# Splitting the expert-weight loads of a one-core hybrid decoder step into halves, with a new cut of the last two units and one filler less

## The reference

```python
logits = (xt @ w_router + b_router).astype(jnp.float32)
top_v, top_i = lax.top_k(logits, TOP_K)          # 4 of 32
gates = jax.nn.softmax(top_v, axis=-1)
...
gu = xb @ w_gate_up[e] + b_gate_up[e]            # 1024 -> 2048
gate, up = gu[:, :D_EXPERT], gu[:, D_EXPERT:]
gate = jnp.minimum(gate, SWIGLU_LIMIT)
up = jnp.clip(up, -SWIGLU_LIMIT, SWIGLU_LIMIT)
act = (up + 1.0) * (gate * jax.nn.sigmoid(SWIGLU_ALPHA * gate))
return act @ w_down[e] + b_down[e]               # 1024 -> 1024
```

## Time and profile before

| | before |
|---|---|
| time, median of 3 runs | 1357.94 us (1357.71 to 1358.34) |
| profiled execution, its own time | 1358.47 us |
| its span, first to last instruction | 1356.8 us |
| TensorE busy | 1318.4 us, 97% |
| queue q1 (SP): bytes, share of 16 DMA engines | 460.21 MB, 84.0% |
| HBM read | 477.33 MB |
| mean granted TensorE clock | 0.996 |

### The profile page before, as it was taken

One profiled execution on the slowest core, in us unless ns is written; L12 is line 12 of the kernel. 1 busy time (PEld: TensorE's weight loads), 2 busy tenths in 40 slices (PEclk: granted clock), 3 DMA queues, 4 the chain that ended last, 5 costly groups with the idle time before them and its releaser, 6 DMA issues.

```text
span 1356.8 us, 16732 instructions
## 1 busy us (share of the span) xinstructions
PE 1318.4 (97%) x6850; PEld 728.7 (54%) x6850; DVE 417.3 (31%) x1089; ACT 258.0 (19%) x583; POOL 35.6 (3%) x56
## 2 busy tenths in 40 slices
PE   9999999999999999999999999999999999999997
PEld 8888888888887344344443443334334333434433
DVE  3755557885312221212111212112111112212112
ACT  2113374484202111010110110101011010101102
POOL 0000012110000000000000000000000000000000
PEclk9999999999999999999999999999999999999999
DMA  9445449997998999999999999999999999999995
GB/s 253 151 131 159 153 148 273 309 344 252 264 333 337 373 425 418 431 431 431 430 430 431 432 431 427 431 431 432 429 430 431 430 430 431 431 432 429 431 424 206
DMA packets 94709, 489.37 MB, mean 361 GB/s; under 512 B 8673, under 2 KB 73761, under 8 KB 78873
## 3 DMA queue, kind: packets, MB, share of 16 engines
q1 hardware_dynamic: 84896, 460.21, 84.0%
q0 software_dynamic: 4608, 24.41, 5.2%
q10 hardware_dynamic: 5129, 3.66, 1.0%
HBM read 477.33 MB, written 11.19 MB: 360 GB/s over the span
## 4 chain that ended last, share of the span: by engine, by line
PE 71%; DMA 27%; ACTq 0%; DVE 0%; issue 0%; ACT 0%; POOL 0%; SPq 0%; POOLq 0%; DVEq 0%
PE bank L320 70%; DMA plain_conv<-in_w_down 9%; DMA ring<-in_w_down 9%; DMA ring<-in_w_gate_up 6%; DMA plain_conv<-in_w_gate_up 3%; PE bank L971 2%; ACTq L691 0%; ACTq L689 0%; DVE exn L2022 0%; ACT plain_conv L937 0%; ACT ring L695 0%; ACT plain_conv L685 0%; SPq L377 0%; DVE exn L1555 0%; DVE plain_conv L2025 0%
## 5 line engine op out<-in xcount | busy, mean ns | idle before, releaser
L320 PE MATMUL bank<-ring,plain_conv 128*64 128x512 f32 (+1 forms) x1312 | 297.6, 594 | 13.9 <-DMA ring<-in_w_gate_up 13.7
L320 PE MATMUL bank<-exn,ring 128*128 128x264 f32 (+1 forms) x1168 | 262.2, 388 | 0.2 <-DVE exn L1555 0.2
L320 PEld LDWEIGHTS bank<-exn,ring 128*128 128x128 f32 (+1 forms) x1168 | 217.4, 189 | 40.3 <-issue 3.2
L320 PEld LDWEIGHTS bank<-ring,plain_conv 128*64 128x64 f32 (+1 forms) x1312 | 92.3, 137 | 190.3 <-issue 166.1
L320 PE MATMUL bank<-plain_conv 128*64 128x512 f32 (+2 forms) x848 | 185.3, 586 | 9.2 <-DMA plain_conv<-in_w_gate_up 8.8
L320 PE MATMUL bank<-ring,exn 128*64 128x512 f32 x576 | 127.6, 595 | 1.9 <-DMA ring<-in_w_down 1.9
L320 PEld LDWEIGHTS bank<-plain_conv 128*64 128x64 f32 (+2 forms) x848 | 59.3, 138 | 125.2 <-issue 109.0
L1950 DVE TENSOR_TENSOR xT<-xT,bank 128x264 f32<-128x264 f32 x128 | 54.4, 429 | 216.1 <-PE bank L320 214.4
L1956 DVE TENSOR_SCALAR bank<-bank 128x512 f32<-128x512 f32 x31 | 21.7, 700 | 321.1 <-PE bank L320 321.1
L320 PE MATMUL bank<-plain_conv,exn 128*64 128x512 f32 (+1 forms) x422 | 99.9, 590 | 2.1 <-DMA plain_conv<-in_w_down 1.8
L874 ACT ACTIVATE exn<-bank 128x512 f32<-128x512 f32 x31 | 18.5, 598 | 414.7 <-DVE bank L1956 414.7
(11 more groups left out here) (299 smaller groups left out, 842.0 us busy)
## 6 DMA issues: line engine op xcount, KB each, us to landing
ring<-in_w_gate_up SPq DMA_DIRECT2D x35, 4096.0 KB, 39.7
plain_conv<-in_w_gate_up SPq DMA_DIRECT2D x23, 4096.0 KB, 40.2
ring<-in_w_down SPq DMA_DIRECT2D x16, 4096.0 KB, 40.4
plain_conv<-in_w_down SPq DMA_DIRECT2D x11, 4096.0 KB, 39.0
ring<-in_w_in SPq DMA_DIRECT2D x36, 1024.0 KB, 5.4
ring<-in_w_gate_up SPq DMA_DIRECT2D x8, 2048.0 KB, 12.0
ring<-in_w_proj_b SPq DMA_DIRECT2D x8, 1024.0 KB, 9.9
plain_conv<-in_w_gate_up SPq DMA_DIRECT2D x4, 2048.0 KB, 12.5
```

The lines of the kernel that those rows point to most:

```text
L320: return nc.tensor.matmul(out, w, x, start=start, stop=stop)
```

## The change

Units 3 to 93 are all loaded in halves of 2 MB, each half issued when the half that it overwrites has been used. Units 94 and 95 come in four pieces of two rows each (1 MB, 8 KB in each partition), alternating between the two, instead of a half and two pieces by columns. TensorE takes them two rows at a time for both halves of the columns, and the last two rows for the left columns and then the right. The filler at line 1225 is removed.

```diff
-SPLIT = range(3, 11)
-HALVES = [sum(n % PLACES == q for n in (*SPLIT, 93)) for q in range(PLACES)]
+SPLIT = range(3, 94)
+ROWS_EACH = (48, 48, 32)
+HALVES = [sum(n % PLACES == q for n in SPLIT) for q in range(PLACES)]
...
-            def load_pair(p, m, q, first=0, split=(), final=False):
+            def load_pair(p, m, q, final=False):
                 j = PLACES * m + q
-                for c in range(first, UNITS):
+                for c in range(UNITS):
                     n = (q + c) % PLACES
                     used = 2 * UNITS * PAIRS * p + 2 * UNITS * j + 2 * (c - PLACES)
-                    if c in split or final and c == 3:
-                        for h in range(2):
-                            sp.wait_ge(S["w_used"], used + 1 + h)
-                            second = half_landed[n]
-                            load_half(j, c, n, h, second if h else unit_landed[n])
+                    if final and c >= 4:
+                        sp.wait_ge(S["w_used"], used + 2)
+                        load_rows(j, c, n, 0, 2, unit_landed[n])
                         continue
+                    sp.wait_ge(S["w_used"], used + 1)
+                    load_half(j, c, n, 0, unit_landed[n])
                     sp.wait_ge(S["w_used"], used + 2)
-                    if final and c >= 4:
-                        load_half(j, c, n, 0, unit_landed[n])
-                    else:
-                        load_unit(j, c, n)
+                    load_half(j, c, n, 1, half_landed[n])
                 if final:
-                    for h in range(2):
+                    for r in range(1, 4):
                         for c in (4, 5):
-                            load_columns(j, c, (q + c) % PLACES, h, columns_landed[h])
+                            load_rows(j, c, (q + c) % PLACES, 2 * r, 2 * r + 2, rows_landed[r - 1])
...
             pe.wait_ge(S["u_taken"], 2)
-            keep_busy(p_first[0], 2)
             pe.wait_ge(S["mark_ready"], 2)
...
                 def second_half(c):
                     n = UNITS * q + c
-                    if isinstance(m, int) and m == 0 and n in SPLIT:
-                        half_arrived(n % PLACES, 1 + sum(o % PLACES == n % PLACES for o in SPLIT if o < n))
-                    if final and c == 3:
-                        half_arrived(3, HALVES[3])
+                    if isinstance(m, int) and m == 0 and n < SPLIT[0]:
+                        return
+                    half_arrived(n % PLACES, UNITS * m + n // PLACES + (n % PLACES >= SPLIT[0]))
...
-                down_both(range(4), range(2), lambda x: arrived(4 + x))
-                down_both(range(4, KT), [0], columns_of(0)).then_inc(S["y_half"], 1)
-                down_both(range(4, KT), [1], columns_of(1)).then_inc(S["w_used"], 4)
+                down_both(range(2), range(2), lambda x: arrived(4 + x))
+                for r in (1, 2):
+                    down_both(range(2 * r, 2 * r + 2), range(2), rows_of(r))
+                down_both(range(6, KT), [0], rows_of(3)).then_inc(S["y_half"], 1)
+                down_both(range(6, KT), [1], rows_of(3)).then_inc(S["w_used"], 4)
```

More of the change, by code:

```diff
@@ L305, in build @@
         half_landed = [sem(f"half_landed{i}") for i in range(PLACES)]
-        columns_landed = [sem(f"columns_landed{i}") for i in range(2)]
+        rows_landed = [sem(f"rows_landed{i}") for i in range(3)]
         dve_step, pool_step = sem("dve_step"), sem("pool_step")
@@ L385, in load_rows @@
                 sp.dma_start(unit[n][:, D * r0:D * r1], unit_of(j, c)[:, r0:r1, :].rearrange("p s n -> p (s n)")).then_inc(landed, 16)
-            def load_columns(j, c, n, h, landed):
-                dst = unit[n][:, HALF:BIG].rearrange("p (s n) -> p s n", s=4)
-                sp.dma_start(dst[:, :, 512 * h:512 * h + 512], unit_of(j, c)[:, 4:8, 512 * h:512 * h + 512]).then_inc(landed, 16)
             for w, k in ((a["w_proj_a"], KT), (a["w_proj_b"], 2 * KT), (a["w_out"], KT)):
@@ L450, in load_pairs @@
                 sp.wait_ge(S["w_used"], 2 * UNITS * PAIRS * p + 2)
-                load_rows(0, 5, 0, 6, 8, columns_landed[1])
-                load_pair(p, 0, 1, split=range(5))
-                for q in range(2, PLACES):
+                load_rows(0, 5, 0, 6, 8, rows_landed[1])
+                for q in range(1, PLACES):
                     load_pair(p, 0, q)
@@ L1380, in down @@
                         if first and x and s == 2:
-                            pe.wait_ge(columns_landed[0], 48 * p + 16)
+                            pe.wait_ge(rows_landed[0], 48 * p + 16)
                         if s == 4:
@@ L1384, in down @@
                         if first and x and s == 6:
-                            pe.wait_ge(columns_landed[1], 48 * p + 16)
+                            pe.wait_ge(rows_landed[1], 48 * p + 16)
                         for half in range(2):
@@ L1400, in down_both, with rows_of @@
                     return ins
-                def columns_of(half):
+                def rows_of(r):
                     def landed_of(x):
-                        pe.wait_ge(columns_landed[half], 48 * p + 48)
+                        pe.wait_ge(rows_landed[r - 1], ROWS_EACH[r - 1] * (p + 1))
                         return unit[(q + 4 + x) % PLACES]
```

2 lines of the change are left out of this document (1 added, 1 removed).

## The result

The changed kernel takes 1364.42 us (median of 5 runs, 1361.87 to 1365.02) beside 1358.31 us for the kernel before (5 runs, 1357.71 to 1359.27). The ratio is 1.004, with a 95% interval of 1.0029 to 1.0051: slower by 6.1 us, or 0.4%. Forecast was 1364.5 us, in a range of 1360.2 to 1368.1. All ten executions lie inside the range, but the close match of the first median is luck: the terms of the sum were off by 1.2 to 2.1 us each, and the errors offset each other.

What follows compares the result with a forecast made beforehand. The DMA engines were taken to bound the kernel from 518 to 1311 us, TensorE after. Terms + 8.0 - 0.4 - 0.45 - 0.55 = + 6.6 us on a median of 1357.94 gave 1364.5 us, range 1360.2 to 1368.1.

Steps and rivals of the forecast that it cites:

- What bounds the kernel: From 518 to 1311 us the DMA engines' rate of moving units sets the time; after 1311 us TensorE does.
- Price of the halves: 82 newly halved units, 11 to 92, each cost 98 ns more per engine: + 8.0 us, bounds 4.8 and 10.7.
- estimate of 4.7 ns: Cost per extra packet worked out from the Trainium skill: 3.1 us for 656 extra packets of an engine.
- a time near 1359.6: Rival: the skill's cheaper packets end the sum at 1359.6 us; anything between 1355.9 and 1360.2 got 14 in 100.
- fixed 2 us: Rival: each transfer pays its own fixed time, serially 164 us for 82 more transfers; 1 in 100.
- What finer issue gives back: Halves issued earlier help only where the DMA queue ran dry, 504 to 518 us: - 0.4 us, bounds 0 and 1.4.
- the dry stretch: 504 to 518 us, DMA share 0.98 and 389 GB/s: 0.3 us lost by share, 1.4 by rate; 0.4 taken.
- The filler: Without the filler at 434.52 us, the gather, first units and DMA stream come earlier: - 0.45 us, bounds 0 and 0.65.
- The rival with the clock: TensorE's clock falls in the last two units, where there is no slack: 1.7 us more, 1366.2 us; 8 in 100.
- The end: After unit 92, the last pieces' landing decides; down matmuls end at 1352.0 us, 0.55 us less than the stream's delay.
- TensorE's lead: Sign: TensorE's lead over the arriving units is gone before 822 us.
- The first expert matmul: Sign: it starts 0.45 us earlier than 439.67 us.

Runs made afterwards that it cites:

- second measurement: The changed kernel run once more, nothing altered, for its spread and a second trace: 1360.82 us (5 runs) beside 1357.68 before, ratio 1.0035.

## Why the prediction was right, and where its terms were off

**What bounds the kernel: right.** From some 510 us the DMA engines set the time. Two kernels that differ from before only in the size of their packets end later by what the packets cost, to within 0.6 us (+ 6.8 where 656 x 9.4 ns are 6.2, + 17.95 where 1968 x 9.3 ns are 18.3).

**Price of the halves: mechanism right, size too high.** The term was + 8.0 us, 12.2 ns per extra packet. Measured are 9.4 ns, which is 82 x 8 x 9.4 = 6.2 us, and + 6.8 us for the whole kernel with smaller packets alone. The step that was mis-sized is the multiplication by the DMA share: a share over 100% over 770 us can hardly be anything but packets that overlap, and it makes small packets look dearer. The same working gives 13 ns per extra packet for those of 8 KB (1.010 x 12320 us for 40756 - 1235 packets), where the kernel's time rose by 17.95 / 1968 = 9.1 ns for each. By bytes, the row that the prediction priced from gives 45 x 16 x 0.032768 / 19.20 = 1228.8 ns against 1219.0, 9.8 ns. The estimate of 4.7 ns that was worked out after the Trainium skill, DMA: Bandwidth & Descriptors, section Why small descriptors are slow (HBM only), is half of what the runs show, and its rival, a time near 1359.6, did not come. The Trainium skill, DMA: Bandwidth & Descriptors, section Anatomy of one DMA, gives its fixed 2 us, from which the prediction made a rival, for the path of GpSimd's transfers, and these go by SP's; nothing of that size shows here (1229.1 against 1228.4 ns with twice the transfers).

**What finer issue gives back: too small.** The terms were - 0.4 for the dry stretch and - 0.55 at the end, together - 0.95 us. Packets alone cost + 6.8 us, halves with the same packets and filler + 4.45 (1362.07 against 1357.62): 2.35 us come back. With the old end the halves cost + 5.4 (1363.00), so about 1.4 us come back without the new end and up to 0.9 with it. The first part holds the dry stretch, for which the rate's bound of 1.4 us may have been nearer than the share, and TensorE following the last gate-and-up units by halves. How these two divide was not measured.

**The filler: wrong in kind.** The term was - 0.45 us, with "idle of a few tenths in their place I cost at nothing". Where the clock holds, the gain is there and larger than forecast: about 0.6 us in the traces (8.77 us from the router's 0.79 us group to the first expert matmul before, 438.77 - 430.62 = 8.15 in the second trace of the changed kernel). The lower group of the changed kernel, near 1360.7, lies 1.4 us under the one with the filler back. But in the first trace the clock falls right behind the filler's place, and by the two groups about half the executions do the same and end near 1364.4. The rival with the clock was written for the tail, at 1.7 us and 8 in 100. The fall came at the head, where TensorE's first matmuls free the places that the stream waits for: the DMA share is 0.48 instead of 0.78 from 436 to 444 us in the two traces, and the whole stream of units comes later. Between the two traces lie 3.8 us. The fall accounts for 3.0 of them; why the halves of unit 93 came another 0.8 us late is open.

**How the sum met the first median.** Against the times of before beside each, the packets cost + 6.8 instead of + 8.0, finer issue and the new end gave back 2.35 instead of 0.95, and the missing filler cost 6.1 - 4.45 = + 1.7 instead of - 0.45. Together this is + 6.1 beside the forecast + 6.6. The first two errors alone would have put the time 2.6 us under the forecast; the fall of the clock, which the sum lacked, made up for most of it. In the second measurement, with three of five executions in the lower group, the slow-down of 3.1 us is about half the forecast. (The low end of the range is 1357.94 + 2.2 = 1360.1, not 1360.2; nothing hangs on it.)

The Trainium skill, TensorE: Matmul & The Clock Gate, section Part 1: The HAM clock gate (the "warmup" mystery), gives the lower clock as that of an idle engine, and says of the rise from it that its moment varies between executions of one kernel. The traces here agree that executions of one program differ, for the fall too: with the filler gone it is there in one (0.57) and not in another (1.00). They differ from it in that TensorE wasn't idle but busy 4.64 of the 6 us ahead of the fall, where it was busy 5.21 with the filler. The kernel without either filler was busy 3.75 there, fell in its one trace and took 1362.75 us against 1357.68. All ten traces with both fillers have 1.00 from 436 to 444 us; of the four with one or both gone, two show a fall. That is the evidence for the fillers holding the clock; it is good but thin, as the kernel before without this one filler was no slower beyond the noise (ratio 1.0005) and didn't fall in its trace.

**The end: right in its lengths, lucky in its times.** Gate-and-up was forecast to end at 1331.9 and ended at 1331.54; the down matmuls at 1352.0, and ended at 1351.37, 5.97 us after those of before. These times hold for the execution with the fall, which the forecast didn't have; without it they are 1327.68 and 1347.49. The lengths are right in both: the last piece was forecast 20.1 us behind unit 93's second half and came 1347.79 - 1327.95 = 19.8 us behind it, 19.8 also without the fall, and the wait before the last two rows is there, 0.62 us. The engines don't end together, which a rate over the whole stretch hides:

```profile
1340.00:1345.00 5.00, 5.00 (x26) 1.72 (x24) 0.00 (x0) 0.00 (x0) 0.00 (x0) 1.00 0.58 243
1345.00:1350.00 5.00, 4.38 (x24) 1.39 (x20) 0.00 (x0) 0.24 (x1) 0.00 (x0) 1.00 0.22 87
```

While the last piece is still under way, until 1347.79, the mean share of the 16 engines falls to 0.58, then 0.22: most of them are done, and the last ones set the landing. The new end alone makes no difference (ratio 1.0006), as what it could cure was hidden; once the halves have made the stream late it is worth up to 0.9 us.

**What was to be seen.** Three signs were wrong. TensorE's lead is not gone before 822 us but after: the chain holds matmuls up to 878 us. This belongs to the halves and not to the clock, since it is 875.80 us without the fall, and 823.77 in the kernel with whole units and the fall. A likely reason is that the last piece of TensorE's wait is now a half unit, so that a lead of the same bytes lasts longer. The first expert matmul came at 440.13 in the first trace, 0.46 us later than before and not 0.45 earlier; without the fall it came at 438.77. And SP is still held at the last pieces, four times for 3.46 to 4.25 us. It costs nothing: the last piece was issued at 1314.72, 13 us before the second half of unit 93, which stands ahead of it in the queue, was there.

## What to carry to other kernels

When a DMA queue never runs dry and the cut makes the packets smaller, it moves no byte earlier and adds the cost of more packets (here 9.4 ns for each extra one); halve only the transfers that come where the queue is empty or where the consumer waits for the last one. Price packets by bytes over time, not by a busy share over 100%. A matmul that computes nothing may be worth more than its time: before removing one, look at what the clock does behind it in several executions, since a single trace or a single median can show either of two outcomes. And set the time of a traced execution beside the median before giving the trace's cause for the whole of a difference: without both fillers the trace explains 2 of 5 us.

## What the runs showed of the hardware

An extra packet costs the same at the sizes tried here: 9.4 ns for one extra in 32 KB (16 KB each), 9.3 ns each for three (8 KB each). A transfer's two or four runs that touch on both sides were sent as packets of 32 KB. A program's granted clock at one place can differ from execution to execution after the same activity (0.57 and 1.00 behind 4.64 busy us of 6). The ten times of that program stand in two groups whose medians are 3.8 us apart; a fall of the clock delays TensorE by 3.0 of the 3.8 us between the two that were traced. The 16 engines don't end a row of transfers together: their mean share is 0.58 and then 0.22 while the last one is still under way.
